# Merge of three mixers: feature tiles 2 to 7 as paired seven-product blocks in place of plain matmuls

## What is computed

```
u = h @ w_in                                     # gates are 3 x 1024 of its columns
m = sum_i sigmoid(gate_i) * (branch_i @ wo_i)    # merge: this change
h = LN(alpha*h + m @ w_out)
h = LN(alpha*h + MoE(h))                         # 64 experts, top 8, one shared
```

## Time and profile before

| what | us |
|---|---|
| median of three runs | 1496.13 |
| the profiled execution, its time | 1495.74 |
| its span, first to last instruction | 1493.9 |
| TensorE busy | 1447.2 (97% of the span) |
| VectorE busy | 667.6 (45%) |
| ScalarE busy | 406.9 (27%) |
| GpSimd busy | 179.6 (12%) |
| merge, from the first part behind the last GLA chunk to `w_out` | 760.8 to 887.1 |

### The profile page before, as it was taken

How to read it: one execution, slowest core, us unless ns; L and a number is a source line. 1 busy time by engine, 2 the same in 40 slices (tenths; PEclk the granted TensorE clock), 3 DMA queues, 4 the chain that set the end, 5 groups by cost and what they waited for, 6 DMA issues and landing times.

```text
span 1493.9 us, 31845 instructions
## 1 busy us (share of the span) xinstructions
PE 1447.2 (97%) x13359; PEld 1031.0 (69%) x13359; DVE 667.6 (45%) x1258; ACT 406.9 (27%) x920; POOL 179.6 (12%) x155
## 2 busy tenths in 40 slices
PE   7999999999999999999999999999999999999995
PEld 6997766777776777777666766776575767676751
DVE  7445787875735777634531124522212121121227
ACT  2335435344234444335421101111111111111111
POOL 3771212122010000000000000000101000010000
PEclk9999999999999999999999999999999999999998
DMA  7787457263245445563677548599999999999984
GB/s 279 192 158 175 157 146 210 83 212 113 92 118 162 117 114 152 186 194 109 190 230 237 144 135 357 209 378 402 418 425 428 428 428 428 427 428 428 427 348 188
DMA packets 157037, 375.31 MB, mean 251 GB/s; under 512 B 101724, under 2 KB 110316, under 8 KB 139232
## 3 DMA queue, kind: packets, MB, share of 16 engines
q1 hardware_dynamic: 140928, 345.78, 65.0%
q0 software_dynamic: 6576, 16.48, 3.2%
q10 hardware_dynamic: 9392, 11.06, 2.2%
HBM read 327.14 MB, written 51.95 MB: 254 GB/s over the span
## 4 chain that ended last, share of the span: by engine, by line
PE 83%; DVE 6%; DMA 4%; DVEq 2%; issue 2%; ACT 1%; SPq 1%; ACTq 1%
PE PS L648 21%; PE PS L1177 15%; PE PS L1027 8%; PE PS L1196 7%; PE PS L1144 7%; PE PS L665 6%; PE PS L730 3%; PE PS L1149 2%; DVE region L1645 2%; PE PS L1065 2%; DVE region L1638 2%; PE PS L738 1%; DMA region<-w_in 1%; PE PS L1160 1%; PE PS L1185 1%
## 5 line engine op out<-in xcount | busy, mean ns | idle before, releaser
L648 PE MATMUL PS<-h0T,region 128*128 128x320 f32 x1424 | 408.6, 439 | 1.2 <-issue 0.8
L648 PEld LDWEIGHTS PS<-h0T,region 128*128 128x128 f32 x1424 | 264.8, 190 | 115.0 <-issue 13.0
L1280 ACT ACTIVATE region<-PS 128x320 f32<-128x320 f32 (+6 forms) x384 | 147.0, 394 | 647.0 <-PE PS L648 233.4
L1177 PE MATMUL PS<-region 128*64 128x512 f32 x1024 | 228.8, 592 | 0.0
L1177 PEld LDWEIGHTS PS<-region 128*64 128x64 f32 x1024 | 124.4, 137 | 92.2 <-issue 32.0
L1280 ACT ACTIVATE region<-region 128x256 f32<-128x256 f32 (+11 forms) x229 | 99.2, 464 | 157.8 <-DMA region<-projected 39.2
L1027 PE MATMUL PS<-region 128*128 128x320 f32 x512 | 138.6, 433 | 2.8 <-DMA region<-wo 2.7
L1027 PEld LDWEIGHTS PS<-region 128*128 128x128 f32 x512 | 97.0, 190 | 44.0 <-issue 2.4
L1638 DVE TENSOR_TENSOR region<-region 128x256 f32<-128x256 f32 (+10 forms) x188 | 117.6, 647 | 20.6 <-ACTq L1569 4.9
L1280 ACT ACT_TABLE_LOAD x80 | 102.6, 1283 | 72.1 <-DMA region<-projected 55.8
L1196 PE MATMUL PS<-region,history 128*64 128x512 f32 x512 | 119.7, 596 | 0.8 <-ACTq L1600 0.5
(11 more groups left out here) (221 smaller groups left out, 1443.3 us busy)
## 6 DMA issues: line engine op xcount, KB each, us to landing
region<-moe_w SPq DMA_DIRECT2D x64, 2048.0 KB, 18.2
region<-moe_w SPq DMA_DIRECT2D x64, 1024.0 KB, 16.1
region<-w_in SPq DMA_DIRECT2D x115, 512.0 KB, 5.6
region<-wo SPq DMA_DIRECT2D x32, 512.0 KB, 3.7
projected<-region ACTq DMA_DIRECT2D x64, 167.5 KB, 3.7
expert_rows<-region SPq DMA_DIRECT2D x20, 512.0 KB, 6.6
region<-expert_rows SPq DMA_DIRECT2D x5, 2048.0 KB, 13.8
region<-projected SPq DMA_DIRECT2D x10, 768.0 KB, 6.3
```

Source lines behind the costliest of these rows:

```text
L648: last = mm(PS[:, 6 + i % 2, 0:NTOK], WR[:, i, k, :], H0T[:, k, :], start=(k == 0), stop=(k == KT - 1))
L1177: last = mm(PS[tiles(i), 2, :], XE[:, k, tiles(i)], W13[r][i][:, k * 512:k * 512 + 512], start=(k == 0), stop=(k == KT - 1))
L1280: return nc.scalar.activation(out, in_, f, **kw)
```

## The change

Parts of d = 0 and d = 1 stay as they were, except that the part (d = 1, q = 1) now follows directly on (d = 1, q = 3) and goes to bank 5. The 24 parts of d = 2 to 7 become 12 units. Unit u takes two tiles d and d + 1 and one q, in the order q = 0, 2, 3, 1 for each pair of tiles, and runs seven products as `project_pair` does.

- Weights: eight slots for units 0 to 7. Four of them (`WOS`) lie in the place of `w_out`, which is therefore loaded only when unit 5 has read its weights. Units 8 to 11 go through the four slots of `WR`. The loads of units 0 and 1 are issued right after those of d = 0, ahead of the GLA state.
- GpSimd: four sums of 512 columns for each unit (`unit_sums`); four sums of 640 columns of the branch for each q (`token_sums`, three of them, and `token_sum_in_place`), those of q = 0 and 2 in part before the GLA stage, the rest in the merge. The last weight sum of unit 1 waits for `merged` 2, since it is written over the gates of d = 0 and 1.
- ScalarE: unrolled; the gates of d = 0 to 3 first, then a wait for `merged` 2, then four PSUM copies for each unit, with the gates of d = 4 to 7 behind units 1 to 4.
- VectorE: for each unit four additions of 160 columns and two operations of 640 columns.
- SyncE: unrolled; the gates of d = 2 and 3 before the loads of unit 3.

```diff
+        WOS = WOUT.rearrange("p a b -> p (a b)")[:, 0:4 * KT * 128].rearrange("p (r k f) -> p r k f", r=RING, k=KT)
+        def unit_weights(u):
+            if u in (0, 1, 4, 5):
+                return WOS, (2 * (u % 2), 2 * (u % 2) + 1), (u // 4 + PAIRS // 4 + 1) * 16
+            n = {2: 0, 3: 0, 6: 1, 7: 1, 8: 2, 9: 2, 10: 3, 11: 3}[u]
+            return WR, ((0, 2), (3, 1))[u % 2], n
...
             for q in MIX_ORDER:
                 mixer_weights(0, q, NT)
+            for u in range(2):
+                load_unit(u, (NT, NT))
             gla_out(0)
...
             gates(0, 0)
-            merge_weights(1, STEP_ORDER[:2])
+            load_unit(2, (NT + 4, NT + 5))
             gates(1, 1)
-            merge_weights(1, STEP_ORDER[2:])
-            sp.dma_start(WOUT, io['w_out']).then_inc(sem("w_out_in"), 16)
-            with sp.Fori(1, 3) as d2:
-                for p in range(2):
-                    merge_loads(d2 * 2 + p, p)
...
+            mixer_weights(1, 1, NT + 6)
+            for d in (2, 3):
                 sp.wait_ge(sem("gates_ready"), d)
+                gates(d, d % 2)
+            load_unit(3, (NT + 7, NT + 8))
+            for u in range(4, UNITS):
+                if u == 8:
+                    sp.wait_ge(sem("tile_done"), freed(5))
+                    sp.dma_start(WOUT, io['w_out']).then_inc(sem("w_out_in"), 16)
+                old = u - 4 if u < 8 else u - 2
+                load_unit(u, (freed(old), freed(old)))
+                if u < 8:
+                    sp.wait_ge(sem("gates_ready"), u)
+                    gates(u, u % 2)
...
+            def merge_unit(u):
...
+                pe.wait_ge(sem("quads_out"), p + 1)
+                product(X, lambda k: ring[:, a, k, :], lambda k: OTS[q][:, k, 0], True)
+                product(Z, lambda k: ring[:, b, KH + k, :], lambda k: MSUM[q][3][:, k], True)
+                pe.wait_ge(sem("weights_summed"), p + 1)
+                pe.wait_ge(sem("quad_kept"), p * 4 + 1)
+                product(X, lambda k: S2[:, k], lambda k: MSUM[q][1][:, k], False)
+                pe.wait_ge(sem("quad_kept"), p * 4 + 2)
+                product(Z, lambda k: ring[:, a, KH + k, :], lambda k: OTS[q][:, KH + k, 0], True)
+                product(W, lambda k: S1[:, k], lambda k: MSUM[q][0][:, k], True)
+                pe.wait_ge(sem("quad_kept"), p * 4 + 3)
+                product(X, lambda k: S3[:, k], lambda k: MSUM[q][2][:, k], False, True)
+                pe.wait_ge(sem("quad_kept"), p * 4 + 4)
+                product(W, lambda k: S4[:, k], lambda k: OTS[q][:, KH + k, 1], False)
...
-            for q in STEP_ORDER:
-                merge_part(1 + (q != 1), q, MERGE_BANKS[q == 1][q])
...
+            merge_part(1, 1, 5)
+            for u in range(UNITS):
+                if u < 2:
+                    pe.wait_ge(sem("merged"), u + 1)
+                if u < 4:
+                    pe.wait_ge(sem("token_sums"), u + 2)
+                merge_unit(u)
...
-                if k == KT - 1:
+                if k == KT - 2:
                     pe.wait_ge(sem("merged"), 8)
...
+            for d in range(4):
+                open_gates(d)
+            act.wait_ge(sem("merged"), 2)
+            for u in range(UNITS):
+                X, Z, W = (PS[:, 3 * (u % 2) + x, 0:160] for x in range(3))
+                act.wait_ge(sem("quads_out"), PAIRS + u + 1)
+                keep_unit(u, 1, 0, X)
+                keep_unit(u, 2, 2, Z)
+                keep_unit(u, 3, 1, X)
+                keep_unit(u, 5, 3, W)
+                if 1 <= u <= 4:
+                    open_gates(u + 3)
...
+            def unit_out(u):
...
+                tt(part(0), part(0), Z, add)
...
+                for x in (2, 3):
+                    tt(part(x), part(x), X, add)
+                dve.wait_ge(sem("quad"), 7 * p + 7)
+                tt(part(1), part(1), W, add)
...
+                tt(K, K, gate, mul)
+                dve.drain()
+                tt(out, out, K, add)
+                dve.drain().then_inc(sem("quads_out"), 1)
+                if q == UNIT_ORDER[3]:
+                    nc.vector.sem_inc(sem("merged"), 2)
```

More of the change, by code:

```diff
@@ L38 @@
 PAIRS = (PRE - RING) // 2
+UNITS = 12
+UNIT_ORDER = (0, 2, 3, 1)
+GATE_OF = (8, 0, 16, 16)
 HEAD_R, FILL = 4, 8
@@ L1034, in _, with product @@
             pe.wait_ge(sem("phase_over"), ENG * 4)
-            def merge_step(d, p):
-                pe.wait_ge(sem("merged"), d)
-                for q in STEP_ORDER:
-                    merge_part(d + (q != 1), q, (MERGE_BANKS[p] if q == 1 else MERGE_BANKS[1 - p])[q])
+            def merge_unit(u):
+                p, q = PAIRS + u, UNIT_ORDER[u % 4]
+                ring, (a, b), _ = unit_weights(u)
+                X, Z, W = (PS[:, 3 * (u % 2) + x, 0:160] for x in range(3))
+                S1, S2, S4, S3 = USUM[u % 2]
+                def product(out, lhs, rhs, start, freed=False):
+                    for k in range(KH):
+                        last = mm(out, lhs(k), rhs(k), start=start and k == 0, stop=k == KH - 1, skip_group_check=True)
+                        if freed and k < 2:
+                            last.then_inc(sem("tile_done"), 1)
+                    last.then_inc(sem("quad"), 1)
+                for i in (a, b):
+                    pe.wait_ge(sem(unit_in(u, i)[0]), unit_in(u, i)[1])
+                pe.wait_ge(sem("quads_out"), p + 1)
[11 more added lines that the diff above has]
+                product(W, lambda k: S4[:, k], lambda k: OTS[q][:, KH + k, 1], False)
@@ L1043, in _ @@
             merge_part(0, 1, 1)
             merge_part(1, 3, 4)
-            for q in STEP_ORDER:
-                merge_part(1 + (q != 1), q, MERGE_BANKS[q == 1][q])
-            with pe.Fori(1, 3) as d2:
-                for p in range(2):
-                    merge_step(d2 * 2 + p, p)
-            merge_step(6, 0)
-            merge_part(7, 1, MERGE_BANKS[1][1])
-            pe.wait_ge(sem("merged"), 7)
+            merge_part(1, 1, 5)
[5 more added lines that the diff above has]
+                merge_unit(u)
@@ L2150, in _ @@
             merge(0, (6, 1, 7), NT + 6)
-            with dve.Fori(0, 3) as d2:
-                for p in range(2):
-                    merge(d2 * 2 + (p + 1), MERGE_BANKS[1 - p], d2 * 8 + (4 * p + NT + 10))
-            merge(7, MERGE_BANKS[1], NT + 32)
+            merge(1, MERGE_BANKS[1], NT + 8)
+            def unit_out(u):
+                p, (d, q) = PAIRS + u, unit_feature(u)
+                X, Z, W = (PS[:, 3 * (u % 2) + x, 0:160] for x in range(3))
+                K = UKEPT[u % 2]
+                part = lambda x: K[:, 160 * x:160 * x + 160]
+                dve.wait_ge(sem("quad"), 7 * p + 4)
+                dve.wait_ge(sem("quad_kept"), 4 * p + 1)
+                tt(part(0), part(0), Z, add)
+                dve.wait_ge(sem("quad"), 7 * p + 6)
+                dve.wait_ge(sem("quad_kept"), 4 * p + 4)
+                for x in (2, 3):
[3 more added lines that the diff above has]
+                dve.drain()
+                dve.wait_ge(sem("gates_ready"), d + 3)
+                gate = GTF[:, d + GATE_OF[q]:d + GATE_OF[q] + 2, :].rearrange("p a b -> p (a b)")
+                out = MG[:, d:d + 2, :].rearrange("p a b -> p (a b)")
+                if q == UNIT_ORDER[0]:
+                    tt(out, K, gate, mul)
+                    dve.drain().then_inc(sem("quads_out"), 1)
+                    return
+                tt(K, K, gate, mul)
+                dve.drain()
+                tt(out, out, K, add)
+                dve.drain().then_inc(sem("quads_out"), 1)
+                if q == UNIT_ORDER[3]:
+                    nc.vector.sem_inc(sem("merged"), 2)
+            for u in range(UNITS):
+                unit_out(u)
             dve.wait_ge(sem("ln_in"), 64)
```

122 lines of the change are left out of this document (100 added, 22 removed).

## The result

The changed kernel takes 1501.74 us (median of 16 runs, 1497.05 to 1505.44) against 1495.50 for the kernel before in the same jobs (16 runs, 1492.48 to 1498.12). The ratio is 1.0035 with a 95% interval of 1.0026 to 1.0045, about 5 us slower. The prediction was 1494.8 with a range of 1489.5 to 1499.5: the time lies outside it, on the slower side, to which the prediction had given 0.15.

A forecast was written before the change was run, and what follows sets the result against it. The prediction took the stage to be bound by TensorE's work: 13.3 us less against waits of 3.0 + 2.0 + 5.9 + 1.2 more made 1.3 less, a median of 1494.8 us, range 1489.5 to 1499.5.

The forecast's parts named there:

- TensorE's own work: In the merge, 24 parts and a gap of 1.0 us give way to 12 units of 7.62 us: 13.3 us less.
- The state load: Last GLA chunk: four loads of 512 KB ahead of the state make TensorE wait 3.0 us, bounds 0 and 5.
- The part (1, 1): Fifth part of the merge, d = 1, q = 1: TensorE waits 2.0 us for its load, bounds 1 and 3.
- No wait in units 4 to 7: Sign of being right: from unit 4 on GpSimd's sums need 5.6 of each 7.6 us and are in time.
- VectorE is no bound: Units of the merge: VectorE takes 7.3 us a unit at most, under TensorE's 7.62, so no rival of its own.
- The gates of d = 4 to 7: ScalarE in the merge: these gates have a whole unit each.
- `w_out` in front of unit 8: Rival, chance 0.12: unit 8's weights land late behind `w_out`, TensorE waits 7.2 us instead of 1.2; together 6.6 more, 1501.4.
- the four waits: TensorE's waits: state load 3.0, part (1, 1) 2.0, GpSimd at units 2 and 3 5.9, unit 8 1.2 us.
- the sum: Balance up to the start of `w_out`: 13.3 us less against 3.0 + 2.0 + 5.9 + 1.2 more, 1.3 less.
- GpSimd's chain: Start of the merge, queued sums through unit 3: 27.9 us plus 0.5 beside VectorE; TensorE waits 5.9, bounds 4 and 8.
- the 1.2: Unit 8: TensorE waits 1.2 us for sums of weights that land behind `w_out`, bounds 0 and 8.
- ScalarE: Unit 0: gates of d = 2 and 3 delay the first copy, some 1.3 us, costing nothing ahead of GpSimd's wait.

The follow-up runs named there:

- the four loads alone: Kernel before with only four loads of 512 KB put ahead of the GLA state, into the place of `w_out`: 1501.13 us, ratio 1.0022.
- the filled wait: Changed kernel with the first product of unit 3 repeated three times into an unread bank ahead of the wait for GpSimd: 1499.64 us, ratio 1.0029.
- the best kernel: Changed kernel with loads of units 0 and 1 behind the state, (1, 1) before unit 2, `w_out` halved, GpSimd and ScalarE reordered: 1483.14 us, ratio 0.9916.
- the run with ScalarE's order alone: Changed kernel with only the gates of d = 2 and 3 and the wait for `merged` 2 moved to unit 1: 1499.27 us, ratio 1.0025.
- the run with the state ahead: Changed kernel with the loads of units 0 and 1 issued behind the GLA state instead of ahead of it: 1502.63 us, ratio 1.0027.

## Why the prediction was wrong

**Right, by its own steps.** TensorE's own work: -13.3 was said, and 12.66 are gained where next to nothing waits; a pair costs 7.62 us in the merge as in the projection (1.09 for eight records in both). The spacing in the Trainium skill (TensorE: Matmul & The Clock Gate, Back-to-back issue gap), from which the prediction estimated 0.8 of the price of 320 columns for 160, does not hold for these float32 matmuls: the trace has 0.136 against 0.270 us. The state load: 3.0 was said, 2.8 came, 3.02 with the four loads alone. The part (1, 1): 2.0 against 1.75. No wait in units 4 to 7, nor between unit 8's and the end. VectorE is no bound; its operations of 640 columns between SBUF operands take 0.83 us alone and up to 1.75 beside GpSimd's, 0.9 more where the prediction took 1.27. The gates of d = 4 to 7 are in time. `w_out` in front of unit 8 was named as the rival on the slower side, with a landing of unit 8's weights 13 us after their issue; they landed 7.3 us behind it (issued at 850.45, GpSimd's first sum at 857.77), as the forecast had it (7.2):

```profile
850.45 26.23 SPq L567 DMA_DIRECT2D region<-wo  x8
...
857.77 1.27 POOL L2694 TENSOR_TENSOR region<-region 128x512 f32<-128x512 f32 x1 [7.04 <-DMA region<-wo]
...
862.22 1.84 POOL L2701 TENSOR_TENSOR constants<-region 128x512 f32<-128x512 f32 x1
```

So that rival did not decide, nor did any other of them. That its time, 1501.4, is near the measured 1501.74 is a coincidence.

**The step that failed: the clock.** The prediction added up waits against a TensorE whose records always last 0.136 or 0.270 us; the four waits were priced at their length and nothing more. In every profile with waits of 2 us or more but one (the kernel before with four loads added), at least one of them goes with a stretch in which the granted clock is at half, and the records take up to twice as long. In the profile of the changed kernel this is 2.8 us in two places, the largest single part of what the sum lacked, and it would have turned -1.3 into +1.5. The waits themselves, sized too low by 2.6 in all (below), are nearly as much; with either alone the time would have stayed inside the range (1498.9 or 1499.1, an estimate from these two terms). The upper end of the range had room for longer waits and none for this. That the clock has a price of its own is shown by the filled wait: with the same sums at the same time, 16 records took 2.44 us in place of 4.00. That it goes with the waits fits the best kernel, without long waits and with a clock of 1.00 throughout the stage. From run to run the time goes with the clock: of the 16 runs of the changed kernel the three slowest, 1504.5 to 1505.4, have a mean of 0.989, the four fastest, 1497.1 to 1497.9, have 0.993 or 0.994. That the change makes the kernel less steady is not shown: its runs spread over 8.4 us, those of the kernel before over 5.6 in the same jobs and 5.9 to 8.7 in the later ones.

**Sized too low: GpSimd's chain.** From the last sum of unit 1 to the end of unit 3's sums 27.9 + 0.5 = 28.4 us were said, and 30.0 came (791.89 to 821.87). The stretching beside VectorE was taken as 0.5; it is 2.1:

```profile
796.74 1.54 POOL L2673 TENSOR_TENSOR h0T<-region,h0T 128x640 f32<-128x640 f32 x1
798.43 2.22 POOL L2675 TENSOR_TENSOR h0T<-region,h0T 128x640 f32<-128x640 f32 x1
...
805.43 1.27 POOL L2698 TENSOR_TENSOR region<-region 128x512 f32<-128x512 f32 x1
806.65 1.85 POOL L2701 TENSOR_TENSOR constants<-region 128x512 f32<-128x512 f32 x1
```

An operation of 512 columns takes 1.27 us alone and up to 1.85 beside one of VectorE's with 640 columns, one of 640 takes 1.54 or up to 2.22. The same at unit 8: its four sums take 857.77 to 864.06, 6.3 us in place of the 5.6 said, which is over half of the 1.2 by which that wait was said too short. All waits together were 14.7 against 12.1 said; 2.6 of the miss is here and 2.8 is the clock.

**Right in size, wrong in cause: ScalarE.** The prediction had this wait at 0.8 us by its times, "some 1.3" in its words, and 0.98 came. The gates of d = 3 were named as the late ones. They were there and the sigmoid was over at 790.2; what the first copy waited for was `merged` 2:

```profile
789.21 1.00 ACT L1353 ACTIVATE region<-region 128x960 f32<-128x960 f32 x1 [1.18 <-DMA region<-projected]
791.84 0.71 ACT L1353 ACTIVATE history<-PS 128x160 f32<-128x160 f32 x2 [1.64 <-DVEq L2239]
```

The prediction compared 787.3 with `merged` 2 at 786.8 and took the later one; the order was the other way round. In the changed kernel it cost nothing either way (the run with ScalarE's order alone).

**Open.** A further stretch of slower clock lies at the start of the expert stage. There every profile has the same wait of TensorE for VectorE, 1.06 to 1.08 us, with the same 24 records behind it. In the changed kernel:

```profile
954.39 10.67 PE L1201 MATMUL PS<-region,h0T 128*128 128x512 f32 x24 [1.07 <-DVEq L2358]
```

and in the kernel before:

```profile
948.87 8.97 PE L1128 MATMUL PS<-region,h0T 128*128 128x512 f32 x24 [1.06 <-DVEq L2236]
```

In the profiles of the changed kernel and of six others the 24 records take 10.67 us, 1.7 more, and in those of the kernel before and of the remaining six 8.97. It is there with `w_out` in two halves and with it in one piece, and no experiment was aimed at it; the prediction had no term for it either. Nor is it settled why `w_out` in two halves gave 5.8 us by the ratios.

## What to carry to other kernels

A block product with seven of eight multiplications gives its eighth back nearly in full (here 12.7 of 13.3 us) where sums, copies and loads are all there before TensorE asks, and nothing or less where they are not: with the same matmuls the program took 1501.7 us in one order of the helper queues and loads and 1483.1 in another. In the queue of a helper engine a wait that comes late has to stand last among the operations that don't need it, and moving a load ahead of another may do no more than move the wait, as the run with the state ahead shows. Price a wait of a nearly full TensorE at its length plus what the records behind it may lose at the lower clock (1.1 to 1.7 us here, in 16 of 25 cases), and where such waits are more than one, let the range reach to the slower side for it.

## What the hardware showed that was not expected

- Waits of TensorE of 2 to 4 us in this stage often go with some 3.4 us at half the clock, which costs 1.1 to 1.7 us; in one case it was 6.8 us and cost 2.7. Of the 25 waits of 1.95 us or more in this stage, over all profiles of the study, 16 had it, among them all eight over 3.1 us; nine, between 2.12 and 3.02, had not.
- The length of a wait alone does not tell. The same wait at unit 8 had the slower clock in one profile (2.19) and not in another (2.33), and a wait of 1.07 us at the start of the expert stage had it in 7 of 14 profiles.
- The lower clock does not begin where the wait ends. In windows of half a microsecond it begins at 760.3 for the wait that ends at 760.03, 1.4 us behind the wait's end in another profile (821.6, wait to 820.18), and 1.3 us ahead of it in a third (860.0, wait to 861.28).
- Matmuls that nobody reads, in the place of a wait, cost nothing at unit 3 (from the part (1, 1) to the product behind the wait 37.24 us with them, 37.22 without) and kept the records behind them fast: 32 in the window of 4 us behind the wait, where the changed kernel has 18.
- GpSimd is stretched by VectorE too, not only VectorE by GpSimd: 1.27 us become up to 1.85, 1.54 up to 2.22. In a chain of eighteen operations that was 2 us.
